# Hybrid decoder layer with a mixture of experts: expert rows written first as residual plus contribution, then added, through two row lists and three token buffers

## The chip, the cores and the metric

One core of one Trainium2 chip. The metric is the device time of one execution in microseconds (us), median of three runs. All arithmetic is float32. The engines are TensorE (PE in the profile, PEld its weight loads), VectorE (DVE), ScalarE (ACT), GpSimd (POOL) and SyncE (SP). Transfers are carried by the core's 16 DMA engines. SP issues the weight loads; POOL issues the indirect ones, whose row numbers lie in SBUF.

## What is computed

One layer on 512 tokens of width 1024: RMSNorm, one input projection whose columns feed a Mamba-2 head group and a forgetting-attention head group, an output projection, and a residual sum, called x2 here. Then the part that matters:

```python
g_star = jnp.argmax(grp_logits, axis=-1)               # one of 4 groups of 8 experts
top_val, top_idx = lax.top_k(sel, 2)                   # two experts of that group
w2 = jax.nn.softmax(top_val, axis=-1) * p_g
hid = silu(h @ w_gate[e]) * (h @ w_up[e])              # 1024 -> 256, for each chosen expert e
x = x2 + sum over the token's two experts of w2 * (hid @ w_down[e])
```

There are 32 experts with 3 MB of weights each. Every token has exactly two contributions, both from one group of eight experts.

## The kernel before, in words

**Up to the router.** x2 is made in blocks of 128 tokens (chunks). SP writes each chunk twice to DRAM: to `x2_dram`, from which rows are gathered, and to the output, to which contributions are added (lines 476 and 477). DVE routes the tokens (`route_group`, `route_first`, `route_second`, from line 1885): `i1` and `i2` are keys of a token's two experts (the larger key is the lower expert number), and `E12` is their one-hot form. Each expert has `CAP` = 64 slots. PE turns one-hot products into a token number for each slot (`slot_tokens`, line 1394) and DVE stores them as `slot_rows` (line 1965), with `NO_ROW`, out of bounds, where a slot is empty. PE then sums how many slots each expert holds (lines 1436 to 1438) and makes the gate weight and the norm scale of each slot (line 1445).

**The expert stage.** There are 16 pairs: pair p is expert p on partitions 0 to 63 and expert p + 16 on partitions 64 to 127. A pair's work is:

- `gather(p)` (POOL, line 682): 128 slot rows of 4 KB from `x2_dram` into one of two buffers of `xg`.
- `tokens_transpose(p)` (PE, line 1456), then `tokens_copy(p)` (ACT line 1017 and DVE line 1994) into `xgT`.
- `gate_up(p)` (PE, line 1483; lines 1472 for pairs 0 and 1): 32 matmuls. `gate(p)` (ACT, line 1024) and `gated(p)` (DVE, line 2001) make `hid`; `hid_transpose(p)` (PE, line 1492) and `hidT_store(p)` (DVE, line 2008) turn it.
- `down(p)` (PE, line 1507): 16 matmuls into PSUM banks 6 and 7.
- `rows_scale(p)`: ACT scales the front half of the result (line 1030) while DVE scales the back half (line 2014) into `yrow`.
- `scatter(p)` (POOL, line 698): adds the 128 rows to the output in DRAM. It waits until the scatter of pair p-1 has landed, since two pairs can hold the same token.

SP loads the weights: three buffers for gate and up (4 MB a pair, line 367), four for down (2 MB a pair, line 383). A load into a buffer waits for `gate_up` or `down` of the pair that used it last.

What sets the order is the program of each engine. PE's loop is written so (`AHEAD` is 12):

```python
for p in range(NPAIR):
    if p < AHEAD: gate_up(p + 1, p + 1)
    hid_transpose(p)
    if p < NPAIR - 2: tokens_transpose(p + 2, p % 2)
    down(p, p)
    if AHEAD <= p < NPAIR - 1: gate_up(p + 1, p + 1)
```

DVE does in a step `hidT_store(p)`, `gated(p+1)`, `tokens_copy(p+2)`, `rows_scale(p)`; from p = 12 `gated(p+1)` comes last. ACT does `gate(p+1)`, `tokens_copy(p+2)`, `rows_scale(p)`. POOL issues gathers 0 to 3, then in step p `gather(p+4)` and `scatter(p)`; `gather(p)` waits for `tokens_transpose(p-2)`, which frees its buffer. After the loop all engines read `most_i`, the fullest expert's count; more rounds of a slower loop would follow only if it were over 64.

Of the kernel before, what the change touches and what calls it, by code (L numbers as in the profile page):

```python
# [20 lines left out]
P = 128  # L21
# [24 lines left out]
NGU, NDN = 3, 4  # L46
# [36 lines left out]
def hybrid_layer(nc, x, norm_mix_w, w_in, conv_w, conv_b, dt_bias, a_log, d_skip, ssm_norm_w, q_norm_w, k_norm_w,  # L83
# [7 lines left out]
    with ExitStack() as ctx:  # L91
# [17 lines left out]
        def sem(name):  # L109
            if name not in sems:  # L110
# [7 lines left out]
                         [("dn1", [P, 2, 2, D], F32), ("gu1", [P, 2, 2, KC, DE], F32)]))  # L118
# [26 lines left out]
                         [("sg", [P, DE], F32), ("hid", [P, DE], F32), ("hidT", [P, 2, DE], F32), ("yrow", [P, 2, D], F32),  # L145
                          ("slot_rows", [P, NPAIR], I32), ("slot_scale", [P, 2, NPAIR], F32), ("slot", [P, 4, 4], I32)],
# [14 lines left out]
                         + [(n, [P, TC, H], F32) for n in ("ncum", "ecum", "dte", "etot")], [("turn", [P, NE], F32)]))  # L161
        sp, lf, cum, tot, ncum, ecum, dte, etot = (m[n] for n in ("sp", "lf", "cum", "tot", "ncum", "ecum", "dte", "etot"))
        turn = m["turn"]
# [22 lines left out]
        slot_rows, slot_scale = m["slot_rows"], m["slot_scale"]  # L186
        slot = m["slot"]
# [196 lines left out]

        def more_experts(eng, expert):
# [12 lines left out]
        def _(sp):  # L398
# [123 lines left out]
            for j in range(2):
                sp.wait_ge(sem(f"rows_out{j}"), 16 * (NPAIR // 2))
# [3 lines left out]
        def _(pool):  # L527
# [8 lines left out]
            def lows(first, end):  # L536
                for i in range(first, end):
                    if low_engine("w", i) == "pool":
# [5 lines left out]
                               pattern=[[-1, P]], channel_multiplier=1).then_inc(sem("const_ident"), 1)  # L544
            pool.memset(ones[:], 1.0).then_inc(sem("const_ones"), 1)
            lows(0, HL)

            pool.wait_ge(sem("const_ident"), 1)
            pool.wait_ge(sem("const_ones"), 1)

            pool.affine_select(out=tri[:], in_=ones[:], compare_op=ALU.is_ge, fill=0.0, base=0,
                               pattern=[[1, P]], channel_multiplier=-1).then_inc(sem("const_masks"), 1)

            pool.affine_select(out=stri[:], in_=ones[:], compare_op=ALU.is_gt, fill=0.0, base=0,
                               pattern=[[1, P]], channel_multiplier=-1).then_inc(sem("const_masks"), 1)
# [21 lines left out]
            last.then_inc(sem("const_masks"), 1)  # L577
# [64 lines left out]
            for n in range(N_SO, N_AO):  # L642
                for k in range(KC):
# [6 lines left out]
                    if n == N_AO - 1 and k == 0:  # L650
# [4 lines left out]
                               1.0 / P, None, ALU.mult).then_inc(sem("turn_set"), 1)  # L655
# [26 lines left out]
            def gather(p):  # L682

                j = p % 2
                if p >= 2:
                    pool.wait_ge(sem("xg_transposed"), p - 1)
                pool.indirect_dma_start(out=m["xg"][:, j, :], out_offset=None, in_=x2_dram[:, :],  # L687
                                        in_offset=bass.IndirectOffsetOnAxis(ap=slot_rows[:, p:p + 1], axis=0),
                                        bounds_check=T - 1, oob_is_err=False).then_inc(sem(f"xg_in{j}"), 16)
# [12 lines left out]
            def gather_more(p, r4, n, row):  # L702

                j, e = r4 % 2, p % NPAIR
                pool.wait_ge(sem("xg_transposed"), p - 1)
                pool.wait_ge(sem(f"rows_out{j}"), (p - j) * 8)
                pool.wait_ge(sem("y_scaled_act"), p - 1)
                pool.wait_ge(sem("y_scaled_dve"), p - 1)
# [12 lines left out]
            def scatter_more(p, r4, n):  # L721

                j = r4 % 2
                pool.wait_ge(sem(f"rows_out{1 - j}"), (p + j) * 8)
                pool.wait_ge(sem("y_scaled_act"), p + 1)
                pool.wait_ge(sem("y_scaled_dve"), p + 1)
# [10 lines left out]
            gather(3)  # L737
            for p in range(NPAIR):
                if p + 4 < NPAIR:
                    gather(p + 4)  # L740
                scatter(p)
            pool.wait_ge(sem("most_known"), 1)
            over_cap = pool.value_load(most_i[0:1, 0:1])
            with pool.If(over_cap > CAP):
# [7 lines left out]
                for j in range(2):  # L752
                    pool.wait_ge(sem(f"rows_out{j}"), 16 * (ROUNDS * NPAIR // 2))
# [3 lines left out]
        def _(act):  # L757
# [267 lines left out]

            def rows_scale(p, j, gates):
                act.wait_ge(sem("down_done"), p + 1)
                if not isinstance(p, int) or p >= 2:
                    act.wait_ge(sem(f"rows_out{j}"), (p - j) * 8)
                act.activation(m["yrow"][:, j, 0:BLK], ps[6][:], ACT.Copy, scale=gates).then_inc(sem("y_scaled_act"), 1)  # L1030
# [10 lines left out]
            for p in range(NPAIR):  # L1041
# [4 lines left out]
                rows_scale(p, p % 2, slot_scale[:, 0, p:p + 1])  # L1046
# [6 lines left out]
        def _(pe):  # L1053
            pe.wait_ge(sem("const_ident"), 1)
# [13 lines left out]
            def rstd_rows():  # L1068

                pe.wait_ge(sem("const_ones"), 1)  # L1070
# [78 lines left out]
            def small_cums():  # L1149
                pe.wait_ge(sem("logs_known"), 1)  # L1150
                pe.wait_ge(sem("const_masks"), 2)
                pe.wait_ge(sem("const_ones"), 1)
# [4 lines left out]
            def small_rows():  # L1157
                pe.wait_ge(sem("parts_known"), 1)
                pe.wait_ge(sem("const_masks"), 3)
# [215 lines left out]
            def ranks(c):  # L1375
# [4 lines left out]
                if c == 0:  # L1380
                    pe.wait_ge(sem("turn_set"), 1)
# [67 lines left out]
            def tokens_transpose(p, j):  # L1449
                pe.wait_ge(sem(f"xg_in{j}"), (p - j) * 8 + 16)  # L1450
# [3 lines left out]
                rows = m["xg"][:, j, :].rearrange("t (p k) -> t k p", k=KC)  # L1454
# [40 lines left out]
            def down(p, r4):  # L1495
# [3 lines left out]
                if not isinstance(p, int) or p >= 1:  # L1499
                    pe.wait_ge(sem("y_scaled_act"), p)  # L1500
                    pe.wait_ge(sem("y_scaled_dve"), p)
# [14 lines left out]

            tokens_transpose(0, 0)
            gate_up(0, 0)
            for p in range(NPAIR):
# [12 lines left out]
        def _(dve):  # L1532
# [432 lines left out]
            dve.tensor_scalar(slot_rows[:], ps[5][:, 0:NPAIR], float(NO_ROW), None, ALU.add).then_inc(sem("rows_known"), 1)  # L1965
            for k, at in ((0, i1), (1, i2)):
# [13 lines left out]
            dve.wait_ge(sem("slots_done"), 2)  # L1980
# [3 lines left out]
            dve.wait_ge(sem("ranks_done"), TC + 1)  # L1984
            dve.tensor_reduce(most[:], ps[6][:, 2 * NE:3 * NE], AX, ALU.max).then_inc(sem("dve_seq"), 1)
            dve.wait_ge(sem("dve_seq"), step())
            dve.tensor_copy(most_i[:], most[:]).then_inc(sem("most_known"), 1)
# [21 lines left out]

            def rows_scale(p, j, gates):  # L2010
                dve.wait_ge(sem("down_done"), p + 1)
                if not isinstance(p, int) or p >= 2:
                    dve.wait_ge(sem(f"rows_out{j}"), (p - j) * 8)
                dve.tensor_scalar(m["yrow"][:, j, BLK:], ps[7][:], gates, None, ALU.mult).then_inc(sem("y_scaled_dve"), 1)  # L2014
# [9 lines left out]
            gated(0, 0, slot_scale[:, 1, 0:1])  # L2024
            for p in range(NPAIR):
# [5 lines left out]
                rows_scale(p, p % 2, slot_scale[:, 0, p:p + 1])  # L2031
# [27 lines left out]
```

## Time and profile before

| what | value |
|---|---|
| time, median of 3 runs | 774.24 us (773.31 to 775.62) |
| the profiled execution: its own time | 774.24 us |
| its span, first to last instruction | 772.6 us |
| busy: PE, DVE, ACT, POOL | 709.6, 380.6, 279.3, 145.4 us |
| DMA bytes in the span | 150.31 MB |
| read from and written to HBM | 145.09 MB, 12.88 MB |
| expert stage, first gather issued | 519.5 us |
| last matmul of the last pair ends | 763.5 us |

Busy time is the sum over instructions of an engine; a busy PE is not PE at its peak, since matmuls overlap. PEclk is the share of its full clock that TensorE was granted. DMA share is the mean busy share of the 16 DMA engines. Times inside the trace count from the start of the span. In the list of instructions a bracket behind a row gives the engine's idle time before it and what ended it.

### The profile page before, as it was taken

Reading aid. Unit: us, or ns where it says so; the run is one execution under the profiler, and the core shown is the slowest. Engines: PE = TensorE matmul, PEld = TensorE weight load, DVE = VectorE, ACT = ScalarE, POOL = GpSimd, SP = SyncE. Lnnn points to the kernel's source line nnn. Section 1 sums busy time; section 2 is a strip of 40 time slices with the busy share of each in tenths; the row PEclk is TensorE's granted clock in tenths of the full one; section 3 lists DMA queues with packets and bytes.
Section 4 is the critical chain, followed back from the end, with each engine's and each line's share of the span. In section 5 each row is a group of like instructions: output and inputs, shape, how many; then the busy total and the mean of one; then the engine's idle time right before and its main releaser. Section 6 shows DMA issues by size and latency. Waiting matters only on the chain.

```text
span 772.6 us, 10496 instructions
## 1 busy us (share of the span) xinstructions
PE 709.6 (92%) x3892; PEld 476.4 (62%) x3892; DVE 380.6 (49%) x758; ACT 279.3 (36%) x648; POOL 145.4 (19%) x126
## 2 busy tenths in 40 slices
PE   6999999999999999999999999988999786868784
PEld 5867888788888888666566688876433232323221
DVE  6876777785868723766776553471212110111100
ACT  4934633544454445544554432221212110211100
POOL 3513331330301102000120032011122111111111
PEclk9999999999999999999999999977999898989988
DMA  8333212330303122500110059798999999999972
GB/s 279 84 110 109 92 36 93 108 95 14 108 3 109 53 88 78 212 8 1 52 59 2 1 197 419 316 375 316 407 402 404 393 407 416 404 413 408 387 281 42
DMA packets 44038, 150.31 MB, mean 195 GB/s; under 512 B 11557, under 2 KB 11649, under 8 KB 32209
## 3 DMA queue, kind: packets, MB, share of 16 engines
q1 hardware_dynamic: 38384, 134.61, 45.5%
q0 software_dynamic: 4720, 8.70, 4.6%
q10 hardware_dynamic: 880, 6.30, 2.0%
q8 instruction: 33, 0.54, 0.3%
q14 instruction: 21, 0.16, 0.1%
HBM read 145.09 MB, written 12.88 MB: 204 GB/s over the span
## 4 chain that ended last, share of the span: by engine, by line
PE 67%; SPq 15%; DVE 6%; DMA 6%; ACT 3%; issue 2%; POOL 0%; POOLq 0%; ACTq 0%; DVEq 0%
PE bank L1093 13%; PE bank L1095 12%; PE bank L1094 12%; SPq L367 10%; PE bank L1483 6%; SPq L383 4%; DMA s_gu<-in_w_expert_up_dram 4%; PE bank L1507 3%; PE bank L1330 3%; PE bank L1302 2%; PE bank L1316 2%; PE bank L1472 2%; DVE s_wl L261 2%; PE bank L1210 2%; PE bank L1306 1%
## 5 line engine op out<-in xcount | busy, mean ns | idle before, releaser
L1483 PE MATMUL bank<-s_gu,s_xgT 128*64 128x512 f32 x448 | 110.3, 649 | 29.7 <-DMA s_gu<-in_w_expert_up_dram 29.7
L261 DVE TENSOR_TENSOR s_wl<-s_raw,s_wh 128x512 fp32r<-128x512 f32 x84 | 88.5, 1092 | 25.9 <-ACT s_wh L772 25.6
L1483 PEld LDWEIGHTS bank<-s_gu,s_xgT 128*64 128x64 f32 x448 | 36.6, 149 | 102.2 <-issue 102.2
L772 ACT ACTIVATE s_wh<-s_raw 128x512 fp32r<-128x512 f32 x120 | 74.0, 630 | 41.6 <-PE bank L1095 18.4
L1093 PE MATMUL bank<-s_wh,s_hTh 128*128 128x512 f32 x192 | 78.7, 410 | 0.0
L261 POOL TENSOR_TENSOR s_wl<-s_raw,s_wh 128x512 fp32r<-128x512 f32 x36 | 53.5, 1498 | 131.7 <-ACT s_wh L772 131.1
L1095 PE MATMUL bank<-s_wh,s_hTl 128*128 128x512 f32 x192 | 75.0, 391 | 0.0
L1094 PE MATMUL bank<-s_wl,s_hTh 128*128 128x512 f32 x192 | 74.8, 390 | 0.0
L2008 DVE COPY s_hidT<-bank 128x256 f32<-128x256 f32 x16 | 6.8, 424 | 115.1 <-PE bank L1492 115.1
L1507 PE MATMUL bank<-s_dn,s_hidT 128*64 128x512 f32 x256 | 58.5, 598 | 1.0 <-DVE s_hidT L2008 1.0
L1024 ACT ACTIVATE s_sg<-bank,s_slot_scale 128x256 f32<-128x256 f32 x16 | 7.6, 473 | 138.0 <-PE bank L1483 129.1
L926 ACT ACTIVATE s_Pe<-bank,s_nmax 128x128 f32<-128x128 f32 (+3 forms) x64 | 33.6, 525 | 54.3 <-DVE s_nmax L1805 54.3
L698 POOL DMA_INDIRECT out_dram<-s_yrow,s_slot_rows x16 | 25.2, 1576 | 86.1 <-DVE s_yrow L2014 69.4
L1094 PEld LDWEIGHTS bank<-s_wl,s_hTh 128*128 128x128 f32 x192 | 36.1, 188 | 8.3 <-issue 1.4
L1093 PEld LDWEIGHTS bank<-s_wh,s_hTh 128*128 128x128 f32 x192 | 36.1, 188 | 8.2 <-issue 1.4
L1095 PEld LDWEIGHTS bank<-s_wh,s_hTl 128*128 128x128 f32 x192 | 36.0, 188 | 7.7
L687 POOL DMA_INDIRECT s_xg<-x_rows,s_slot_rows x16 | 16.6, 1037 | 122.5 <-PE bank L1456 119.0
L1093 PE MATMUL bank<-s_hTh,s_wh 128*128 128x512 f32 x96 | 38.4, 400 | 0.0
L1095 PE MATMUL bank<-s_hTh,s_wl 128*128 128x512 f32 x96 | 37.5, 391 | 0.0
L1094 PE MATMUL bank<-s_hTl,s_wh 128*128 128x512 f32 x96 | 37.4, 390 | 0.0
L1507 PEld LDWEIGHTS bank<-s_dn,s_hidT 128*64 128x64 f32 x256 | 17.0, 136 | 30.5 <-issue 27.4
L2014 DVE TENSOR_SCALAR s_yrow<-bank,s_slot_scale 128x512 f32<-128x512 f32 x16 | 12.0, 751 | 48.2 <-PE bank L1507 48.2
(280 smaller groups left out, 1338.4 us busy)
## 6 DMA issues: line engine op xcount, KB each, us to landing
s_dn<-in_w_expert_down_dram SPq DMA_DIRECT2D x30, 1024.0 KB, 23.8
s_gu<-in_w_expert_gate_dram SPq DMA_DIRECT2D x28, 1024.0 KB, 23.1
s_gu<-in_w_expert_up_dram SPq DMA_DIRECT2D x28, 1024.0 KB, 25.7
s_raw<-in_w_in_dram SPq DMA_DIRECT2D x88, 256.0 KB, 3.5
s_raw<-in_w_out_dram SPq DMA_DIRECT2D x32, 256.0 KB, 3.2
s_xin<-in_x_dram SPq DMA_DIRECT2D x4, 512.0 KB, 6.2
s_zs<-in_x_dram SPq DMA_DIRECT2D x1, 2048.0 KB, 10.4
s_gu<-in_w_expert_gate_dram ACTq DMA_DIRECT2D x2, 1024.0 KB, 11.1
```

The source lines that it names most:

```text
L261: eng.tensor_tensor(low, full, high.bitcast(F32), ALU.subtract).then_inc(sem(f"{what}_low_{low_engine(what, i)}"), 1)
L367: sp.dma_start(m[f"gu{b}"][:, half, which, :, :].rearrange("p k f -> p (k f)"), src).then_inc(sem(f"gu_in{b}"), 16)
L383: sp.dma_start(m[f"dn{b}"][:, half, :, :].rearrange("p k n -> p (k n)"), src).then_inc(sem(f"dn_in{b}"), 16)
L698: pool.indirect_dma_start(out=out[:, :], out_offset=bass.IndirectOffsetOnAxis(ap=slot_rows[:, p:p + 1], axis=0), in_=m["yrow"][:, j, :], i ...
L772: act.activation(wh[:, i % HL, :], raw[:, i % RAW, :], ACT.Copy).then_inc(sem("w_high"), 1)
L926: act.activation(Pe[:, v % 3, 0:n], ps[4 + v % 3][:, 0:n], ACT.Exp, bias=nmax[:, v:v + 1], accum_out=rsum[:, v:v + 1]).then_inc(sem("p_exp ...
L1093: pe.matmul(dst, ah, bh, start=start, stop=False)
L1094: pe.matmul(dst, ah, bl, start=False, stop=False)
L1095: return pe.matmul(dst, al, bh, start=False, stop=stop)
L1330: last = pe.matmul(ps[7][par * HD:(par + 1) * HD, qb * P:(qb + 1) * P], V[:, kb, h * HD:(h + 1) * HD], PT[:, par, kb * P:(kb + 1) * P], st ...
L1483: last = pe.matmul(ps[j][r, :].rearrange("p (w f) -> p w f", w=2), m["xgT"][:, j, k, r], gu[:, half, :, k, :], start=(k == 0), stop=(k == ...
L1507: last = pe.matmul(ps[6 + nb][r, :], m["hidT"][:, j, at:at + CAP], dn[:, half, q, nb * BLK:(nb + 1) * BLK], start=(q == 0), stop=(q == 1))
```

## The change

Instead of adding both contributions of a token to the output, the pair that holds a token's first contribution (the lower expert number) writes residual plus contribution plainly; the second contribution is added by a scatter as before.

- DVE marks which of a token's two experts is first (`is_first`, `E_first`); PE makes a second list of slot rows from it (16 matmuls of the kind of line 1399) where it counted slots before; the counting (`totals`) moves behind `gate_up(0)`.
- `rows_split` (DVE, after `gated(0)`) makes `first_rows`, `second_rows` and `holds_first`, a factor of 1 for the slots that hold a first contribution and 0 for the others.
- `keep_first(p)` (ACT) multiplies the gathered rows in place by `holds_first`. `rows_finish(p)` (DVE) then makes `yrow` = matmul result x gate + kept row, both halves one after the other. Pairs 7 and 15 hold no first contribution and keep `rows_scale`.
- `scatter(p)` issues a plain write by `first_rows` (14 pairs) and an adding one by `second_rows` (14 pairs; pairs 0 and 8 hold no second one).
- The gathered rows are needed until `rows_finish`, so there are three buffers, and `gather(p)` waits for the rows of pair p-3. POOL issues gathers 0 to 2, then `gather(p+3)` and `scatter(p)` in step p.

The core of the diff; the waits for constants merely share one semaphore, and the rare extra rounds get new counts:

```diff
             def gather(p):
-                j = p % 2
-                if p >= 2:
-                    pool.wait_ge(sem("xg_transposed"), p - 1)
-                pool.indirect_dma_start(out=m["xg"][:, j, :], out_offset=None, in_=x2_dram[:, :],
+                if p >= NXG:
+                    pool.wait_ge(sem("y_front"), p - NXG + 1)
+                    pool.wait_ge(sem("y_back"), p - NXG + 1)
+                pool.indirect_dma_start(out=token_rows(p), out_offset=None, in_=x2_dram[:, :],
...
             def scatter(p):
                 j = p % 2
                 if p:
-                    pool.wait_ge(sem(f"rows_out{1 - j}"), (p + j) * 8)
-                pool.wait_ge(sem("y_scaled_act"), p + 1)
-                pool.wait_ge(sem("y_scaled_dve"), p + 1)
-                pool.indirect_dma_start(out=out[:, :], out_offset=bass.IndirectOffsetOnAxis(ap=slot_rows[:, p:p + 1], axis=0),
-                                        in_=m["yrow"][:, j, :], in_offset=None, bounds_check=T - 1, oob_is_err=False,
-                                        compute_op=ALU.add).then_inc(sem(f"rows_out{j}"), 16)
+                    pool.wait_ge(sem(f"rows_out{1 - j}"), landed(p - 1))
+                pool.wait_ge(sem("y_front"), p + 1)
+                pool.wait_ge(sem("y_back"), p + 1)
+                if has_first(p):
+                    pool.indirect_dma_start(out=out[:, :], out_offset=bass.IndirectOffsetOnAxis(ap=first_rows[:, p:p + 1], axis=0),
+                                            in_=m["yrow"][:, j, :], in_offset=None, bounds_check=T - 1, oob_is_err=False)\
+                        .then_inc(sem(f"rows_out{j}"), 16)
+                if has_second(p):
+                    pool.indirect_dma_start(out=out[:, :], out_offset=bass.IndirectOffsetOnAxis(ap=second_rows[:, p:p + 1], axis=0),
+                                            in_=m["yrow"][:, j, :], in_offset=None, bounds_check=T - 1, oob_is_err=False,
+                                            compute_op=ALU.add).then_inc(sem(f"rows_out{j}"), 16)
...
             gather(2)
-            gather(3)
+            pool.wait_ge(sem("rows_known"), 3)
             for p in range(NPAIR):
-                if p + 4 < NPAIR:
-                    gather(p + 4)
+                if p + NXG < NPAIR:
+                    gather(p + NXG)
                 scatter(p)
...
+            def keep_first(p):
+                if p == 0:
+                    act.wait_ge(sem("rows_known"), 3)
+                act.wait_ge(sem("xg_transposed"), p + 1)
+                act.activation(token_rows(p), token_rows(p), ACT.Copy, scale=holds_first[:, p:p + 1]).then_inc(sem("first_kept"), 1)
...
-            pe.matmul(ps[6][:, 2 * NE:3 * NE], ones[:], turn[:], start=True, stop=False)
+            pe.wait_ge(sem("rows_known"), 2)
             for c in range(TC):
-                last = pe.matmul(ps[6][:, 2 * NE:3 * NE], ones[:], occ[:, c, :], start=False, stop=(c == TC - 1))
-            last.then_inc(sem("ranks_done"), 1)
+                for k in range(2):
+                    for half in range(2):
+                        last = pe.matmul(ps[7][half * CAP:(half + 1) * CAP, 0:NPAIR], pick_tok(c)[:, k, :],
+                                         E_first[:, k, c, half * NPAIR:(half + 1) * NPAIR], start=(c == 0 and k == 0), stop=(c == TC - 1 and k == 1))
+            last.then_inc(sem("slots_done"), 1)
...
             tokens_transpose(0, 0)
             gate_up(0, 0)
+            totals()
...
+            def rows_finish(p, j, gates):
+                dve.wait_ge(sem("down_done"), p + 1)
+                dve.wait_ge(sem("first_kept"), sum(has_first(q) for q in range(p + 1)))
+                if p >= 2:
+                    dve.wait_ge(sem(f"rows_out{j}"), landed_before(p, j))
+                for nb in range(2):
+                    cols = slice(nb * BLK, (nb + 1) * BLK)
+                    dve.scalar_tensor_tensor(out=m["yrow"][:, j, cols], in0=ps[6 + nb][:], scalar=gates, in1=token_rows(p)[:, cols],
+                                             op0=ALU.mult, op1=ALU.add).then_inc(sem("y_back" if nb else "y_front"), 1)
```

## Rows read from the trace of the kernel before

**Rows 1.** The page, part 2: the span in 40 slices of 19.3 us

```profile
PEclk9999999999999999999999999977999898989988
DMA  8333212330303122500110059798999999999972
```

**Rows 2.** Waits between 500 and 773 us: us in total, times, longest us

```profile
PE bank L1483 <- DMA s_gu<-in_w_expert_up_dram: 29.7, 7, 6.8
```

**Rows 3.** Chain that ended last: start us, us, what

```profile
583.43 6.89 PE bank L1483 x32
590.34 0.33 SPq L367
...
704.18 30.69 DMA s_gu<-in_w_expert_up_dram
735.00 10.07 PE bank L1483 x32
```

**Rows 4.** Instructions of PE in order of time: start us, us

```profile
547.92 7.04 PE L1483 MATMUL bank<-s_gu,s_xgT 128*64 128x512 f32 x32
...
555.23 1.06 PE L1456 MATMUL bank<-s_ident,s_xg 128*128 128x128 f32 x8
...
559.71 7.04 PE L1483 MATMUL bank<-s_gu,s_xgT 128*64 128x512 f32 x32
...
612.20 10.02 PE L1483 MATMUL bank<-s_gu,s_xgT 128*64 128x512 f32 x32 [5.21 <-DMA s_gu<-in_w_expert_up_dram]
...
629.36 7.09 PE L1483 MATMUL bank<-s_gu,s_xgT 128*64 128x512 f32 x32 [2.22 <-DMA s_gu<-in_w_expert_up_dram]
...
699.12 8.78 PE L1483 MATMUL bank<-s_gu,s_xgT 128*64 128x512 f32 x32 [2.52 <-DMA s_gu<-in_w_expert_up_dram]
...
717.57 7.04 PE L1483 MATMUL bank<-s_gu,s_xgT 128*64 128x512 f32 x32
...
726.04 1.06 PE L1456 MATMUL bank<-s_ident,s_xg 128*128 128x128 f32 x8
727.03 3.65 PE L1507 MATMUL bank<-s_dn,s_hidT 128*64 128x512 f32 x16
735.00 10.06 PE L1483 MATMUL bank<-s_gu,s_xgT 128*64 128x512 f32 x32 [4.32 <-DMA s_gu<-in_w_expert_up_dram]
...
750.65 7.04 PE L1483 MATMUL bank<-s_gu,s_xgT 128*64 128x512 f32 x32
```

**Rows 5.** The gathers, pairs 4 to 15 and pairs 0 and 1

```profile
L687 POOL DMA_INDIRECT s_xg<-x_rows,s_slot_rows x12: 988/1042/1047, 545.3 to 710.0; - x12
DMA to landing us min/median/max: 7.8/8.3/9.0
...
DMA to landing us min/median/max: 3.8/3.9/4.0
```

**Rows 6.** Instructions of DVE and POOL: start us, us

```profile
548.14 0.75 DVE L2014 TENSOR_SCALAR s_yrow<-bank,s_slot_scale 128x512 f32<-128x512 f32 x1 [2.90 <-PE bank L1507]
...
549.82 1.62 POOL L698 DMA_INDIRECT out_dram<-s_yrow,s_slot_rows x1 [3.55 <-DVE s_yrow L2014]
```

**Rows 7.** DVE line 1799, ACT line 1000: min/median/max ns, first and last start

```profile
L1799 DVE SCALAR_TENSOR_TENSOR s_zs<-bank,s_rs_a,s_zs x8: 737/751/751, 460.0 to 507.5; 128x512 f32<-128x512 f32 x8
...
L1000 ACT ACTIVATE s_wl<-s_zs x4: 1048/1058/1061, 482.0 to 509.5; 128x1024 fp32r<-128x1024 f32 x4
```

**Rows 8.** PE before the first pair: start us, us

```profile
517.62 0.61 PE L1399 MATMUL bank<-s_E,s_pick_tok 128*64 128x16 f32 x8 [0.34 <-DVE s_pick_tok L1925]
518.17 0.64 PE L1436 MATMUL bank<-s_turn,s_ones 128*128 128x32 f32 x2
518.62 1.89 PE L1438 MATMUL bank<-s_occ,s_ones 128*128 128x32 f32 x8
```

**Rows 9.** Stretches: us; PE, PEld, DVE, ACT, POOL busy; PEclk, DMA share, GB/s

```profile
596.00:600.00 4.00, 4.00 (x22) 1.34 (x20) 0.01 (x1) 0.00 (x0) 1.58 (x1) 1.00 1.03 422
600.00:604.00 4.00, 4.00 (x24) 1.98 (x22) 1.37 (x3) 1.02 (x4) 0.00 (x0) 1.00 1.02 357
...
748.00:752.00 4.00, 4.00 (x22) 1.35 (x20) 0.75 (x1) 0.69 (x1) 0.00 (x0) 1.00 0.27 113
```

More of the change, by code:

```diff
@@ L45 @@
 ROUNDS = T // CAP + 1
-NGU, NDN = 3, 4
+NGU, NDN, NXG = 3, 4, 3
 AHEAD = 12
@@ L383, in load_down, with token_rows, has_first, has_second @@
                 sp.dma_start(m[f"dn{b}"][:, half, :, :].rearrange("p k n -> p (k n)"), src).then_inc(sem(f"dn_in{b}"), 16)
+        def token_rows(p):
+            return m["xg"][:, p % NXG, :] if p % NXG < 2 else m["xg2"][:]
+        def has_first(p):
+            return p % NEG != NEG - 1
+        def has_second(p):
+            return p % NEG != 0
+        def landed(p):
+            return 16 * sum(has_first(q) + has_second(q) for q in range(p % 2, p + 1, 2))
+        def landed_before(p, j):
+            return landed(p - 2) if isinstance(p, int) else (p - j) * 8 + (landed(NPAIR - 1) - 8 * NPAIR)
         def more_experts(eng, expert):
@@ L576, in _ @@
                     pool.wait_ge(sem("pool_seq"), step())
-            last.then_inc(sem("const_masks"), 1)
+            last.then_inc(sem("consts"), 1)
             pool.iota(iota[:], [[1, CAP]], base=0, channel_multiplier=0, allow_small_or_imprecise_dtypes=True)\
@@ L705, in gather_more @@
                 pool.wait_ge(sem("xg_transposed"), p - 1)
[L706 to L708 removed]
+                pool.wait_ge(sem(f"rows_out{j}"), landed_before(p, j))
+                pool.wait_ge(sem("y_front"), p)
+                pool.wait_ge(sem("y_back"), p)
                 held(n)
@@ L1028, in rows_scale @@
                 if not isinstance(p, int) or p >= 2:
-                    act.wait_ge(sem(f"rows_out{j}"), (p - j) * 8)
-                act.activation(m["yrow"][:, j, 0:BLK], ps[6][:], ACT.Copy, scale=gates).then_inc(sem("y_scaled_act"), 1)
+                    act.wait_ge(sem(f"rows_out{j}"), landed_before(p, j))
+                act.activation(m["yrow"][:, j, 0:BLK], ps[6][:], ACT.Copy, scale=gates).then_inc(sem("y_front"), 1)
             def expert_more(p, r4):
@@ L1045, in _ @@
                     tokens_copy(p + 2, p % 2)
-                rows_scale(p, p % 2, slot_scale[:, 0, p:p + 1])
+                if has_first(p):
+                    keep_first(p)
+                else:
+                    rows_scale(p, p % 2, slot_scale[:, 0, p:p + 1])
                 if AHEAD <= p < NPAIR - 1:
@@ L1449, in tokens_transpose @@
             def tokens_transpose(p, j):
-                pe.wait_ge(sem(f"xg_in{j}"), (p - j) * 8 + 16)
+                if isinstance(p, int):
+                    pe.wait_ge(sem(f"xg_in{p % NXG}"), 16 * (p // NXG + 1))
+                    tokens = token_rows(p)
+                else:
+                    pe.wait_ge(sem(f"xg_in{j}"), (p - j) * 8 + (16 * len(range(j, NPAIR, NXG)) + 16 - 8 * NPAIR))
+                    tokens = m["xg"][:, j, :]
                 if not isinstance(p, int) or p >= 1:
@@ L1453, in tokens_transpose @@
                     pe.wait_ge(sem("xgT_dve"), p)
-                rows = m["xg"][:, j, :].rearrange("t (p k) -> t k p", k=KC)
+                rows = tokens.rearrange("t (p k) -> t k p", k=KC)
                 for k in range(KC):
@@ L1515, in expert_more, with totals @@
                 down(p, r4)
+            def totals():
+                pe.matmul(ps[6][:, 2 * NE:3 * NE], ones[:], turn[:], start=True, stop=False)
+                for c in range(TC):
+                    last = pe.matmul(ps[6][:, 2 * NE:3 * NE], ones[:], occ[:, c, :], start=False, stop=(c == TC - 1))
+                last.then_inc(sem("ranks_done"), 1)
             tokens_transpose(0, 0)
             gate_up(0, 0)
+            totals()
             for p in range(NPAIR):
@@ L1965, in _ @@
             dve.tensor_scalar(slot_rows[:], ps[5][:, 0:NPAIR], float(NO_ROW), None, ALU.add).then_inc(sem("rows_known"), 1)
+            dve.tensor_tensor(is_first[:, 0, :], i1, i2, ALU.is_gt).then_inc(sem("dve_seq"), 1)
+            dve.tensor_tensor(is_first[:, 1, :], i2, i1, ALU.is_gt).then_inc(sem("dve_seq"), 1)
+            step()
+            dve.wait_ge(sem("dve_seq"), step())
+            dve.tensor_tensor(E_first[:].rearrange("p k c e -> p (k c) e"), E12[:].rearrange("p k c e -> p (k c) e"),
+                              over(is_first[:].rearrange("p k c -> p (k c)"), P, 2 * TC, NE), ALU.mult).then_inc(sem("rows_known"), 1)
             for k, at in ((0, i1), (1, i2)):
@@ L1983, in _ @@
                 .then_inc(sem("payload_ready"), 1)
[L1984 to L1987, printed above, removed]
             dve.wait_ge(sem("scales_in_slots"), 1)
@@ L2008, in hidT_store, with rows_split, most_slots @@
                 dve.tensor_copy(m["hidT"][:, j, :], ps[4][:, 0:DE]).then_inc(sem("hidT_stored"), 1)
+            def rows_split():
+                dve.tensor_scalar(first_rows[:], ps[7][:, 0:NPAIR], float(NO_ROW), None, ALU.add).then_inc(sem("dve_seq"), 1)
+                dve.tensor_scalar(holds_first[:], ps[7][:, 0:NPAIR], 0.0, None, ALU.is_lt).then_inc(sem("dve_seq"), 1)
+                dve.tensor_scalar(first_away[:], ps[7][:, 0:NPAIR], 0.0, float(NO_ROW), ALU.is_lt, ALU.mult).then_inc(sem("dve_seq"), 1)
+                step()
+                step()
+                dve.wait_ge(sem("dve_seq"), step())
+                dve.scalar_tensor_tensor(out=second_rows[:], in0=ps[5][:, 0:NPAIR], scalar=float(NO_ROW), in1=first_away[:],
+                                         op0=ALU.add, op1=ALU.add).then_inc(sem("rows_known"), 1)
+            def most_slots():
+                dve.wait_ge(sem("ranks_done"), TC + 1)
+                dve.tensor_reduce(most[:], ps[6][:, 2 * NE:3 * NE], AX, ALU.max).then_inc(sem("dve_seq"), 1)
+                dve.wait_ge(sem("dve_seq"), step())
+                dve.tensor_copy(most_i[:], most[:]).then_inc(sem("most_known"), 1)
+            def rows_finish(p, j, gates):
[7 more added lines that the diff above has]
+                                             op0=ALU.mult, op1=ALU.add).then_inc(sem("y_back" if nb else "y_front"), 1)
             def rows_scale(p, j, gates):
@@ L2024, in _ @@
             gated(0, 0, slot_scale[:, 1, 0:1])
+            rows_split()
+            most_slots()
             for p in range(NPAIR):
@@ L2030, in _ @@
                     tokens_copy(p + 2, p % 2)
-                rows_scale(p, p % 2, slot_scale[:, 0, p:p + 1])
+                if has_first(p):
+                    rows_finish(p, p % 2, slot_scale[:, 0, p:p + 1])
+                else:
+                    rows_scale(p, p % 2, slot_scale[:, 0, p:p + 1])
                 if AHEAD <= p < NPAIR - 1:
```

61 lines of the change are left out of this document (31 added, 30 removed).

## The prediction, made before the changed kernel ran

> **What bounds the kernel now.** The page's slices come first. Slices 29 to 38 of 40 (541 to 734 us) all stand at 9 tenths or more of DMA share, so the expert stage is a stream of weights [rows 1]. The waits say the same from PE's side: PE waits 29.7 us for gate and up weights, in 7 waits [rows 2]. The chain that ended last says where it turns: up to 583 to 590 us it runs through PE's matmuls, then through SP's queue, which can't issue faster than the DMA engines drain, until the weights of pair 14 land at 735.0; from there the tail is PE's again [rows 3]. The order of PE's instructions gives two paces. While weights lie ready, a pair takes 559.71 - 547.92 = 11.8 us. Later `gate_up` starts when its weights land, (735.00 - 612.20)/7 = 17.5 us a pair [rows 4]. So between 612 and 735 PE has 5.7 us of slack in each pair, and only DMA time counts. The gathers sit in neither path: POOL issues each one step before PE wants it, and it takes 8.3 us to land [rows 5].
>
> Span 772.6 us, its own time 774.24, which is also the median: I add 1.6 us to a span.
>
> **The change part by part.**
>
> *Less DMA work.* A scatter that adds must read its destination. POOL's 1.58 us between 596 and 600 us is a scatter being issued; in the next 4 us the stream carried 357 GB/s instead of 422 [rows 9]: 65 GB/s x 4 us = 0.26 MB, which is 64 rows of 4 KB, a pair's mean (1024 contributions over 16 pairs). The 512 first contributions lose that reading: 2.1 MB at 0.42 MB/us = 5.0 us of DMA time, nearly all of it before pair 14's weights. Bounds: 0, if a plain write takes as long, and 5.0. The 12 more scatters carry mostly empty slots; their price isn't shown apart, and the dip is used up by the real rows, so I take 0. At most each costs another such dip, 0.26/0.42 = 0.6 us, 7 us in all. All this counts only while DMA sets the pace.
>
> *Before the first pair.* PE's ten counting matmul records (0.64 + 1.89 us) give way to 32 of the kind that took 0.61 us for 8, so 2.4 us, about the same; they return behind `gate_up(0)`, at twice the clock in about 1.1 us (they took 2.3 from the first's start to the last's end) [rows 8]. Small DVE instructions come ahead of the gate weights; the bound covers them. The first gathers are issued as before, and PE's transposes wait for them. I take +1.1 us on PE: `gate_up(2)` starts at 549.0, not 547.92. Bounds 0 and 2.5. Gather 2 is issued earlier and needed later, 0.
>
> *ACT.* `keep_first` is 128x1024, by the row of that size 1.06 us [rows 7], behind `tokens_copy` while PE does `down`, 3.65 us. It ends first; 0. If that cover went, it would add up to 1.06 us a pair, and more would wait for it, as follows.
>
> *POOL.* A step now issues a gather (1.04 us) and up to two scatters (1.6 us each) [rows 5, 6]: 4.2 us out of 15 or more, and `scatter(p)` waits for the landing of p-1, issued a whole step earlier. 0, unless the second scatter lands so late that the next gather queues behind it (below).
>
> *The new wait, which decides.* Now `gather(p+2)` waits until the rows of p-1 are made. Behind it stand, in this order, `tokens_transpose(p+2)`, `down(p)`, the rows of p, and the next gather: a loop, once round per pair. It was open before, since the gather waited for a transpose two pairs back. Its price, from one `gate_up` start (that is when `down` of the pair before is through) to the next:
>
> 1. `down` to DVE's start: 548.14 - 547.92 = 0.2 us [rows 4, 6].
> 2. Rows on DVE alone, both halves: 2 x 0.75 = 1.5 us [rows 7]. Before, ACT did one half beside it.
> 3. DVE's end to POOL's indirect DMA: 549.82 - 548.89 = 0.9 us [rows 6].
> 4. The gather, 8.3 us in a full DMA stream; bounds 3.8 (empty engines) and 9.0 [rows 5]. The stream stays full, so 8.3.
> 5. Transpose and `down`: 559.71 - 555.23 = 4.5 us [rows 4].
>
> Sum 15.4, and some 0.1 of semaphores: 15.5 us a pair instead of 11.8. `gate_up` and the `hid` transpose cover 555.23 - 547.92 = 7.3 us of the first four; PE then stands still for 3.7 us in every pair.
>
> *What the stall does to TensorE's clock.* Idle times of 2.52 and 4.32 us ahead of `gate_up` were followed by one of 8.78 and 10.06 us, against 7.04 at full clock, 2.4 GHz; after 2.22 us there was no loss (7.09) [rows 4]. 3.7 us lies between those that lost 1.7 and 3.0 us to the half clock. Here the transpose and `down` run straight behind the stall, in the loop. I take 1.7 us in three pairs of four, 1.3 us a pair, since short stalls don't always lower the clock. Bounds 0 and 3.0. The loop: 15.5 + 1.3 = 16.8 us.
>
> The Trainium skill, "TensorE: Matmul & The Clock Gate" (HAM oscillation — how this bites in real kernels), has a rule against this change: a loop in which PE waits for a DMA in each trip starts each trip throttled. The rows above agree for single waits; none shows a wait in every trip.
>
> **The sum.** `gate_up` starts behind `down(0)` at 549.0; twelve loops later, with pair 7's half beside ACT (-0.75), `gate_up(13)` starts at 549.0 + 12 x 16.8 - 0.75 = 749.9, against 717.57 before. The slower loop is just under the DMA pace, so the load order keeps running; SP's buffer waits come later, yet its queue had some 20 us of backlog (30.69 us from issue to landing in rows 3). The stream ends about 748 as before [rows 9], or 5 us earlier, and the last gather meets idle engines (3.8 us): PE's own path is longer, 726.04 - 717.57 = 8.5 us to the transpose and 4.6 us to the end of `down(13)`, 763.0 [rows 4]. From `gate_up(14)` to `gate_up(15)` it was 15.65 us with a slow one of 10.06; at full clock 12.6, so 775.6. Behind that start lay 772.6 - 750.65 = 21.95 us: span 797.5, time 799.1 us. The 5 us of DMA time saved are lost to the wait.
>
> **Rivals.**
>
> *A. The loop without a clock loss.* 15.5 us: `gate_up(13)` at 734.3; the last gather is still in the full stream, `down(13)` ends at 749.9; + 12.6 + 21.95 = 784.4, time 786. For: one idle of 2.22 us cost nothing. Against: 2.52 did.
>
> *B. The loop hides, and the change gains.* This is the other side. It needs the loop at 14.6 us or less, which is where the end comes out even: (772.6 - 21.95 - 12.6 + 0.75 - 549.0)/13; so a gather of 7.4 us without clock loss. Below that PE meets the weights in time, and DMA sets the end: 774.2 - 5.0 = 769.2. For: gathers in idle engines took 3.9, and half of the adding falls away. Against: not one of twelve in the stream took less than 7.8, with scatters far from them too.
> The Trainium skill, "DMA: Bandwidth & Descriptors" (Anatomy of one DMA — SWDGE (gpsimd) path), puts a DMA at about 2 us and its bytes over 436 GB/s, 2.6 us for a gather; by that this rival would be the result. The measured 8.3 decides against it.
>
> *C. The gather queues behind the two scatters,* or the clock is lost in full (3.0 us): 18.5 us a loop gives 549.0 + 222 - 0.75 + 13.1 + 12.6 + 21.95 = 817.9, time 819.5. Against: past 17.5 us a pair the weight stream gets gaps, and a gather in a gap is faster; so it is held near 812.
>
> *D. Plain writes save nothing* (the change doesn't do what it says). That alters only B, to 774.
>
> **Numbers.** Forecast 0.60, A 0.22, C 0.05; B 0.08; something between B and A that comes out even 0.05. Range: from 781 (A with 0.4 us less per loop) to 812 (C). A measurement of this kernel can tell 0.3%, 2.3 us. Slower 0.87, same 0.05, faster 0.08.
>
> **What would show it.** Right: gathers preceded by a wait for DVE's line of `rows_finish`, PE's transposes waiting 3 to 4 us for the gather in nearly every pair from pair 3 on, a PEclk below full in most stretches after 550, the weights of pair 14 landing well before PE asks, HBM reads down by 2.1 MB. PE's wait for weights, 29.7 us, would be all but gone. Wrong: `gate_up` still preceded by weight waits near 612 and 735, or gathers landing in under 7.4 us. If the gathers wait but the clock stays full, it is A; if the transposes wait over 5 us, C.

## The result: 802.5 us, 3.6% slower, and the profile after

| | before | after |
|---|---|---|
| time, median of 4 runs each | 774.93 us | 802.53 us (800.90 to 803.23) |
| ratio to before, 95% interval | | 1.0357 (1.0335 to 1.038) |
| the profiled execution: its own time, span | 774.24, 772.6 us | 800.9, 799.3 us |

The forecast was 799.1 us in a range of 781 to 812. One of the six runs of the kernel of experiment 1, below, took 1777 us, for a reason that no trace shows; its ratio leaves that run out. The page of the changed kernel, its head, the rows of slices and the HBM counts:

```profile
span 799.3 us, 10607 instructions
...
PEclk9999999999999999899999999969988999898798
DMA  8333321230311331400200199879999999999412
...
HBM read 145.09 MB, written 19.17 MB: 206 GB/s over the span
```

The DMA row is full to slice 37 (740 us) and then falls to 4, 1 and 2: the weights are in before 750 us, and the kernel runs 50 us longer. Before, the stream ended at about 748 us [rows 9], 24 us ahead of the end. Two rows of the list of waits between 500 and 800 us (us in total, times, longest):

```profile
POOL s_xg L706 <- DVE s_yrow L2087: 169.4, 12, 29.2
...
PE bank L1497 <- DMA s_xg<-x_rows,s_slot_rows: 43.9, 12, 10.0
```

The wait for weights, 29.7 us before [rows 2], is no longer in the list. In its place PE's transposes wait for the gather, twelve times, and the gather waits for the rows that DVE finishes. Two trips round that loop, in the chain that ended last (start us, us, what):

```profile
604.55 0.75 DVE s_yrow L2087
605.42 0.53 issue
606.16 8.37 DMA s_xg<-x_rows,s_slot_rows
614.57 1.20 PE bank L1497 x8
615.77 5.22 PE bank L1548 x16
621.05 0.63 issue
621.68 0.75 DVE s_yrow L2087
623.28 7.80 DMA s_xg<-x_rows,s_slot_rows
```

Rows finished, POOL's reaction, gather, transposes, `down`, and again. `down` took 5.22 us there; in full clock it takes 3.65 [rows 4]. The same in the order of PE's instructions (start us, us; idle time before and its end in brackets), which answers to [rows 4]:

```profile
553.12 7.04 PE L1524 MATMUL bank<-s_gu,s_xgT 128*64 128x512 f32 x32
560.09 0.51 PE L1533 MATMUL bank<-s_ident,s_hid 128*128 128x128 f32 x2
564.40 1.97 PE L1497 MATMUL bank<-s_ident,s_xg 128*128 128x128 f32 x8 [3.80 <-DMA s_xg<-x_rows,s_slot_rows]
566.30 4.37 PE L1548 MATMUL bank<-s_dn,s_hidT 128*64 128x512 f32 x16
570.50 7.03 PE L1524 MATMUL bank<-s_gu,s_xgT 128*64 128x512 f32 x32
...
647.83 1.16 PE L1497 MATMUL bank<-s_ident,s_xg 128*128 128x128 f32 x8 [2.96 <-DMA s_xg<-x_rows,s_slot_rows]
648.91 3.65 PE L1548 MATMUL bank<-s_dn,s_hidT 128*64 128x512 f32 x16
652.40 7.04 PE L1524 MATMUL bank<-s_gu,s_xgT 128*64 128x512 f32 x32
...
744.86 1.97 PE L1497 MATMUL bank<-s_ident,s_xg 128*128 128x128 f32 x8 [9.99 <-DMA s_xg<-x_rows,s_slot_rows]
746.76 4.58 PE L1548 MATMUL bank<-s_dn,s_hidT 128*64 128x512 f32 x16
751.18 7.03 PE L1524 MATMUL bank<-s_gu,s_xgT 128*64 128x512 f32 x32
...
764.13 7.04 PE L1524 MATMUL bank<-s_gu,s_xgT 128*64 128x512 f32 x32
...
776.76 7.04 PE L1524 MATMUL bank<-s_gu,s_xgT 128*64 128x512 f32 x32
```

From `gate_up(2)` to `gate_up(13)` there are twelve trips. They took (751.18 - 553.12)/12 = 16.5 us each, and (717.57 - 547.92)/12 = 14.1 us before, a mean of PE's own pace on a stock of loaded weights and of the weights' pace after it. That is where the time went: 5.2 us by the start of `gate_up(2)`, 28.4 us in the twelve trips, and 6.9 us given back behind `gate_up(13)`, since the weights that PE had to wait for in the end before are now long there (48.1 us to the end instead of 55.0). Together 26.7 us, the difference of the spans.

POOL in one step (start us, us; idle before):

```profile
606.16 1.05 POOL L706 DMA_INDIRECT s_xg<-x_rows,s_slot_rows  x1 [12.12 <-DVE s_yrow L2087]
607.52 1.01 POOL L718 DMA_INDIRECT out_dram<-s_yrow,s_first_rows  x1 [0.31 <-issue]
608.84 1.59 POOL L722 DMA_INDIRECT out_dram<-s_yrow,s_second_rows  x1 [0.30 <-issue]
```

The line of the gathers, pairs 3 to 14, which answers to [rows 5]:

```profile
DMA to landing us min/median/max: 7.6/7.9/8.1
```

The two scatters, of which one is new, take POOL 2.6 us of a step in which it then idles for 12. They stand behind the gather, and no gather took longer for them.

### The profile page after: what moved, and what is told of

Its sections match the earlier page's. It is cut to its first block, busy times and chain, and to the rows that moved or that the text cites. A ratio compares the mean times of both kernels' runs of the same rounds, so it can differ in the third digit from the quotient of the medians.

```text
span 799.3 us, 10607 instructions
## 1 busy us (share of the span) xinstructions
PE 719.0 (90%) x3924; PEld 479.2 (60%) x3924; DVE 390.8 (49%) x779; ACT 284.4 (36%) x648; POOL 156.9 (20%) x138
## 3 DMA queue, kind: packets, MB, share of 16 engines
HBM read 145.09 MB, written 19.17 MB: 206 GB/s over the span
## 4 chain that ended last, share of the span: by engine, by line
PE 71%; DMA 14%; DVE 8%; issue 3%; ACT 3%; POOL 0%; SPq 0%; POOLq 0%; ACTq 0%; DVEq 0%
PE bank L1126 13%; DMA s_xg<-x_rows,s_slot_rows 12%; PE bank L1128 12%; PE bank L1127 12%; PE bank L1548 9%; PE bank L1497 3%; PE bank L1363 3%; PE bank L1524 3%; PE bank L1335 2%; PE bank L1513 2%; PE bank L1349 2%; DVE s_wl L263 2%; PE bank L1243 2%; PE bank L1339 1%; DMA s_raw<-in_w_in_dram 1%
## 5 line engine op out<-in xcount | busy, mean ns | idle before, releaser
L1524 PE MATMUL bank<-s_gu,s_xgT 128*64 128x512 f32 x448 | 98.5, 592 | 0.0
L796 ACT ACTIVATE s_wh<-s_raw 128x512 fp32r<-128x512 f32 x120 | 74.0, 630 | 43.5 <-DMA s_raw<-in_w_in_dram 19.3
L1548 PE MATMUL bank<-s_dn,s_hidT 128*64 128x512 f32 x256 | 71.3, 708 | 1.0 <-DVE s_hidT L2059 1.0
L1524 PEld LDWEIGHTS bank<-s_gu,s_xgT 128*64 128x64 f32 x448 | 31.9, 137 | 64.3 <-issue 64.3
L1497 PE MATMUL bank<-s_ident,s_xg 128*128 128x128 f32 x128 | 22.8, 333 | 43.9 <-DMA s_xg<-x_rows,s_slot_rows 43.9
L1497 PEld LDWEIGHTS bank<-s_ident,s_xg 128*128 128x128 f32 x128 | 18.6, 202 | 46.7 <-DMA s_xg<-x_rows,s_slot_rows 46.1
L1041 ACT ACTIVATE s_xgT<-bank,s_wpk 128x128 f32<-128x128 f32 x64 | 18.3, 368 | 79.0 <-PE bank L1497 79.0
L2087 DVE SCALAR_TENSOR_TENSOR s_yrow<-bank,s_slot_scale,s_xg 128x512 f32<-128x512 f32 x28 | 19.7, 746 | 53.3 <-PE bank L1548 53.3
L1548 PEld LDWEIGHTS bank<-s_dn,s_hidT 128*64 128x64 f32 x256 | 20.0, 163 | 41.4 <-issue 39.0
L2045 DVE TENSOR_TENSOR s_xgT<-bank,s_wpk 128x512 f32<-128x512 f32 x16 | 11.1, 692 | 59.9 <-PE bank L1497 59.9
```

The source lines that it names most:

```text
L796: act.activation(wh[:, i % HL, :], raw[:, i % RAW, :], ACT.Copy).then_inc(sem("w_high"), 1)
L1041: last = act.activation(m["xgT"][:, j, k, :], ps[2][:, k * P:(k + 1) * P], ACT.Copy, scale=wpk[:, k:k + 1])
L1497: last = pe.transpose(ps[2 + k // 4][:, (k % 4) * P:(k % 4 + 1) * P], rows[:, k, :], ident[:])
L1524: last = pe.matmul(ps[j][r, :].rearrange("p (w f) -> p w f", w=2), m["xgT"][:, j, k, r], gu[:, half, :, k, :], start=(k == 0), stop=(k == ...
L1548: last = pe.matmul(ps[6 + nb][r, :], m["hidT"][:, j, at:at + CAP], dn[:, half, q, nb * BLK:(nb + 1) * BLK], start=(q == 0), stop=(q == 1))
L2087: dve.scalar_tensor_tensor(out=m["yrow"][:, j, cols], in0=ps[6 + nb][:], scalar=gates, in1=token_rows(p)[:, cols], op0=ALU.mult, op1=ALU.a ...
```

## The experiments

Each is compared with the kernel before, run on the same chip, which took 774.57 us beside experiments 1 to 4 and 774.33 beside 5 to 7. The changed kernel was not run beside them: what is compared with its 802.53 us, or with times of the other group, goes across separate measurements.

**1. The gather waits only for the kept rows.** ACT writes the kept rows into `yrow`, DVE adds into it in place, and the gather's buffer is free as soon as that copy is made.

```diff
 def gather(p):
-    pool.wait_ge(sem("y_front"), p - NXG + 1)
-    pool.wait_ge(sem("y_back"), p - NXG + 1)
+    pool.wait_ge(sem("xg_transposed"), p - NXG + 1)
+    pool.wait_ge(sem("first_kept"), sum(has_first(q) for q in range(p - NXG + 1)))
...
 def keep_first(p):
-    act.activation(token_rows(p), token_rows(p), ACT.Copy, scale=holds_first[:, p:p + 1])
+    if p >= 2:
+        act.wait_ge(sem(f"rows_out{p % 2}"), landed_before(p, p % 2))
+    act.activation(m["yrow"][:, p % 2, :], token_rows(p), ACT.Copy, scale=holds_first[:, p:p + 1])
...
 def rows_finish(p, j, gates):
-    dve.scalar_tensor_tensor(..., in1=token_rows(p)[:, cols], ...)
+    dve.scalar_tensor_tensor(..., in1=m["yrow"][:, j, cols], ...)
```

> The changed kernel, but ACT writes the kept rows into yrow and the gather waits only for that, not for the finished rows. Theory (the wait of the gather for the finished rows closes a loop that sets the pace): the loop is open again, the weights set the pace, and the 5.0 us of DMA time saved show: 770 us (768 to 773). Rival 1 (more scatters, the rows on DVE alone, or the added work before the first pair set the time): stays near 800. Rival 2 (the loop is open, but plain writes save nothing): 775.

Measured 771.82 us, ratio 0.9966 (0.9953 to 0.9979); once more, beside experiments 5 to 7:

> The version whose gather waits only for the kept rows, unchanged, once more beside the others of this call, as the measure for the one with earlier kept rows: 771.8 us as before (770.5 to 773).

771.14 us, ratio 0.9953 (0.9936 to 0.997). All the lists, scatters, kept rows and DVE's double work are in this kernel, and it is 31 us faster than the changed one. So none of them costs this by itself; what made the loss is the place of the wait, which put them into the loop. Its PE waits for weights again (from the order of PE's instructions, first profile):

```profile
643.34 9.52 PE L1526 MATMUL bank<-s_gu,s_xgT 128*64 128x512 f32 x32 [4.75 <-DMA s_gu<-in_w_expert_up_dram]
...
713.01 1.97 PE L1499 MATMUL bank<-s_ident,s_xg 128*128 128x128 f32 x8 [7.52 <-DMA s_xg<-x_rows,s_slot_rows]
714.91 4.44 PE L1550 MATMUL bank<-s_dn,s_hidT 128*64 128x512 f32 x16
719.19 7.03 PE L1526 MATMUL bank<-s_gu,s_xgT 128*64 128x512 f32 x32
```

One long wait for a gather is left, that of pair 14.

**2. The late gather alone, in the kernel before.** Two buffers suffice for it.

```diff
 def gather(p):
     if p >= 2:
         pool.wait_ge(sem("xg_transposed"), p - 1)
+    if p >= 3:
+        pool.wait_ge(sem("y_scaled_act"), p - 2)
+        pool.wait_ge(sem("y_scaled_dve"), p - 2)
...
 gather(2)
-gather(3)
 for p in range(NPAIR):
-    if p + 4 < NPAIR:
-        gather(p + 4)
+    if p + 3 < NPAIR:
+        gather(p + 3)
```

> The kernel before with one part of the change alone: the gather of pair p also waits for the scaled rows of pair p-3 (POOL issues gather p+3 and scatter p in step p); no lists, no kept rows, no plain writes. Theory: the loop is the whole loss; it is 0.7 us shorter than in the changed kernel since ACT and DVE share the rows: 0.2+0.75+0.9+8.0+0.1+4.5 and 1.4 of clock = 15.9 us a pair, gate_up(13) at 547.9+12x15.9=738.7, and 788 us in all (783 to 793). Rival (the loss lies in the added scatters and DVE work): 775.

Measured 787.66 us, ratio 1.0165 (1.0135 to 1.0196). With nothing else of the change, the wait costs 13 us. Its trips, from the order of PE's instructions:

```profile
549.16 7.04 PE L1485 MATMUL bank<-s_gu,s_xgT 128*64 128x512 f32 x32
...
737.54 7.03 PE L1485 MATMUL bank<-s_gu,s_xgT 128*64 128x512 f32 x32
```

188.4/12 = 15.7 us, against 16.5 in the changed kernel. Of the 0.8 us between them, DVE's second half of the rows is 0.66 (1.41 against 0.75) and the clock 0.34: it cost some 1.7 us in seven of the twelve trips here and in ten there. The gathers of the loop, 8.1 us here and 7.9 there (medians), take 0.2 off. Between the two profiles, 788.0 and 799.3 us long, the twelve trips are 9.7 us; `gate_up(2)` begins 4.0 us later in the changed kernel (553.12 against 549.16), of which 2.4 stand ahead of the first transposes already (526.64 against 524.24), and its tail is 2.3 us shorter. The medians, 787.66 and 802.53, lie further apart, by 14.9 us; the four runs here spread over 6 us.

**3. Filler for PE while it waits.** Matmuls of constants into an unused bank.

```diff
 hid_transpose(p)
+if 1 <= p <= 12:
+    if p == 1:
+        pe.wait_ge(sem("rows_known"), 3)
+    for _ in range(40 if p == 12 else 12):
+        pe.matmul(ps[5][:, 0:P], ones[:], ident[:], start=True, stop=True)
 if p < NPAIR - 2:
     tokens_transpose(p + 2, p % 2)
 down(p, p)
```

> The changed kernel with 12 idle matmuls (40 in step 12) ahead of the transposes of pairs 3 to 14, some 2.6 us of work (9 in step 12) where PE would stand still for the gather. Theory (each stall costs 1.7 us of half clock in the loop): transposes and down take 4.5 us instead of 6.2 in ten of twelve loops, so 12 x 1.45 = 17 us less: 785 us (781 to 790). Rival (the clock's loss falls in cover of the gather and costs nothing): 802 us, or more if the filler itself comes into the path.

Measured 788.76 us, ratio 1.0183 (1.0168 to 1.0198): 13.8 us less, by adding work. First the changed kernel, then the one with filler, in the same stretch (us; busy of PE, PEld, DVE, ACT, POOL; PEclk, DMA share, GB/s):

```profile
560.00:720.00 160.00, 129.66 (x564) 49.02 (x564) 28.51 (x49) 26.18 (x60) 30.70 (x26) 0.91 1.02 410
```

```profile
560.00:720.00 160.00, 152.11 (x851) 75.79 (x849) 29.20 (x50) 28.37 (x65) 33.98 (x28) 1.00 1.02 414
```

The granted clock is 1.00 instead of 0.91, and the order of PE's instructions shows `down` back at its length:

```profile
550.58 7.04 PE L1524 MATMUL bank<-s_gu,s_xgT 128*64 128x512 f32 x32
...
577.31 1.16 PE L1497 MATMUL bank<-s_ident,s_xg 128*128 128x128 f32 x8 [1.39 <-DMA s_xg<-x_rows,s_slot_rows]
578.40 3.65 PE L1548 MATMUL bank<-s_dn,s_hidT 128*64 128x512 f32 x16
...
735.49 7.04 PE L1524 MATMUL bank<-s_gu,s_xgT 128*64 128x512 f32 x32
```

A trip takes 184.9/12 = 15.4 us, 1.1 less. Transposes and `down` take 4.57 us in all twelve trips, against a mean of 5.96: the clock gave 1.4 us, nearly the 1.45 expected. Some came back elsewhere, since the gathers took 8.4 us here (median) and not 7.9.

**4. Plain writes turned into adds, in the kernel with the early gather.**

```diff
 in_=m["yrow"][:, j, :], in_offset=None, bounds_check=T - 1, oob_is_err=False,
+compute_op=ALU.add,
```

> As the first kernel of this call, but the scatter of first contributions adds too instead of writing plainly, so its sums hold the residual twice. Theory (the reading of the destination is real DMA time and shows once the weights set the pace): 5 us over the first kernel, about 775 us. Rival (plain writes and adds cost the stream the same): no difference.

Measured 778.40 us, ratio 1.0047 (1.0031 to 1.0063): 6.6 us over its twin. The two intervals are 0.5% to 1.1% apart, 4 to 8.5 us, so the forecast 5.0 is inside. The stream itself, first with plain writes, then with adds only:

```profile
560.00:720.00 160.00, 133.92 (x618) 51.96 (x615) 31.53 (x54) 28.37 (x65) 38.68 (x32) 0.94 1.02 414
```

```profile
560.00:720.00 160.00, 131.93 (x610) 51.32 (x608) 31.74 (x55) 28.84 (x66) 42.23 (x31) 0.94 1.02 404
```

414 against 404 GB/s at the same full share: 2.5% of a stream of some 200 us, 5 us.

The same run shows what the rest of the change costs once the loop is open. This kernel adds as many rows as the kernel before and takes 3.8 us more (778.40 against 774.57). Some 2.5 of them are likely the last gather's wait (experiment 7). What the 12 more scatters cost is not shown apart: in the window above the kernel before has 406 GB/s against 404 here, which over 200 us is 1 us. So the change as meant saves 5 to 6.6 us, and experiment 1 keeps 2.8 of them.

**5. The same edit in the changed kernel.**

> The changed kernel with its first contributions added instead of written plainly (its sums hold the residual twice); the lists, waits and buffers stay. Theory (the loop of gather, transposes, down and rows sets the pace, so the DMA time saved by plain writes is hidden): 802 to 804 us, like the changed kernel. Rival (the saved DMA time is in the changed kernel's 802.5 us too): 808 us, 6 more, as the version with the early gather showed.

Measured 801.27 us, ratio 1.0341 (1.032 to 1.0363), against 1.0357 (1.0335 to 1.038) with plain writes: no difference; the intervals allow for 4.6 us less and 2.2 us more, and not for 6 more. What is worth 6 us once the weights set the pace is worth nothing inside the loop.

**6. The scatters first, then the gather.**

```diff
 for p in range(NPAIR):
+    scatter(p)
     if p + NXG < NPAIR:
         gather(p + NXG)
-    scatter(p)
```

> The changed kernel with POOL's two lines of a step exchanged: scatter p, then gather p+3. The gather is issued 3.2 us later (1.0 + 1.6 and two gaps of 0.3). Theory (it lies in the loop, once per pair): 11 x 3.2 = 35 us more if the gather takes as long; past 17.5 us a pair the weight stream gets gaps and gathers land faster, so 830 us (822 to 840). Rival (the wait is mostly hidden): under 810 us.

Measured 830.73 us, ratio 1.074 (1.0696 to 1.0784), 28 us more for one exchange of two lines on an engine that is busy a fifth of the time. POOL's step, and the gathers' time to land over all pairs:

```profile
608.30 1.02 POOL L718 DMA_INDIRECT out_dram<-s_yrow,s_first_rows  x1 [15.68 <-DVE s_yrow L2087]
609.63 1.59 POOL L722 DMA_INDIRECT out_dram<-s_yrow,s_second_rows  x1 [0.30 <-issue]
611.52 1.05 POOL L706 DMA_INDIRECT s_xg<-x_rows,s_slot_rows  x1 [0.30 <-issue]
```

```profile
DMA to landing us min/median/max: 3.5/6.3/10.8
```

The gather is issued 3.2 us later. From pair 3 on gathers took 4.0 to 10.8 us to land, 6.7 in the median: the fast ones are as expected once the weight stream has gaps (5.8 us for the one issued at 632.15, with a DMA share of 0.89), the slow ones were not expected (10.8 us for the one issued at 649.93, in a full stream). A trip took 19.0 us ((777.05 - 549.03)/12, the starts of `gate_up(2)` and `gate_up(13)`), 2.5 more than in the changed kernel.

**7. The kept rows of pairs 11 and 12 one step earlier.** The kernel of experiment 1, aimed at its last long wait.

```diff
+if p + 1 in (11, 12):
+    if p + 1 == 11:
+        keep_first(10)
+    keep_first(p + 1)
+elif p in (11, 12):
+    pass
-if has_first(p):
+elif has_first(p):
     keep_first(p)
```

> The version whose gather waits only for the kept rows, with the kept rows of pairs 11 and 12 made one step earlier. In its profile PE stood 7.5 us for the gather of pair 14, in the step that has no gate_up ahead of the transposes, and from there PE's own work set the end. Theory (that stall is what is left of the loss): the transposes of pair 14 wait under 1 us, gate_up(14) meets its weights near 729, 3 us less: 769 us. Rival (the weights land no earlier than PE comes anyway): no difference from 771.8.

Measured 768.64 us, ratio 0.9929 (0.991 to 0.9948), 2.5 us under its twin, measured beside it; the two intervals overlap slightly, so the sign is likely and not certain. The reason was only half right. POOL, then PE:

```profile
698.01 1.59 POOL L722 DMA_INDIRECT out_dram<-s_yrow,s_second_rows  x1 [0.30 <-issue]
699.91 1.05 POOL L706 DMA_INDIRECT s_xg<-x_rows,s_slot_rows  x1 [0.30 <-issue]
```

```profile
712.08 1.93 PE L1505 MATMUL bank<-s_ident,s_xg 128*128 128x128 f32 x8 [4.21 <-DMA s_xg<-x_rows,s_slot_rows]
...
747.98 3.65 PE L1532 MATMUL bank<-s_gu,s_xgT 128*64 128x512 f32 x16 [0.53 <-DMA s_gu<-in_w_expert_up_dram]
```

The transposes of pair 14 still wait 4.2 us, not under 1. Their gather is issued 4.6 us earlier than in experiment 1's first profile (699.91 against 704.55), but right behind the two scatters of pair 10, and takes 12.1 us to land and not 8.4. That it hardly matters is in the last row: the second half of `gate_up(15)` waits for its weights, so this kernel ends with the stream. It is the fastest of all, 6 us under the kernel before.

## Why the prediction was right, step by step

**The wait that decides** was the right one. Experiment 2 has it alone (+13 us), experiment 1 has all but it (-3 us), and experiment 6 makes its loop longer (+28 us). Rival B, the loop hidden, fell: the loop took 16.5 us where it needed 14.6. It nearly came true in experiment 1, once the loop was open: 771.82 and 771.14 us, against its 769.2.

**The terms of the loop**, forecast and measured: rows on DVE 1.5 and 1.41 us; DVE's end to POOL 0.9 and, from 605.30 to 606.16, 0.86; the gather 8.3 and 7.9; transposes and `down` at full clock 4.5 and, where the clock held, 4.57; the clock's loss 1.3 and 1.4. For the last: ten of twelve trips took 6.1 to 6.3 us from the transposes' start to the next `gate_up` (or `hid` transpose), two took 4.57 and 4.58. So the loss was 1.7 us each time it came, as forecast, and it came in ten of twelve trips and not in nine. Rival A, no loss, fell with that, and experiment 3 shows the loss to be in the path. The sum was 16.8 and came out at 16.5.

**The stall** was forecast as 3.7 us. Eleven of the twelve were 2.5 to 3.8 (the twelfth, 10 us, is the step with no `gate_up` ahead of its transposes): the gather was shorter by 0.4 and the rows by 0.1. Even 2.54 us of standing still was followed by a slow `down` of 5.35 us, while the two trips without loss had stood still for 2.96 and 2.90: these rows give no length that decides.

**Rival C**, the gather behind the scatters or the whole 3.0 us of clock, fell: the gather goes first in POOL's step, and the loss was 1.7 us a time. But its cap, the 812 us of the range, was not sound. It rested on faster gathers in the gaps of the stream; experiment 6, which does put the gather behind the scatters, had 19.0 us a trip and 830.73 us.

**The start** was forecast at 549.0 us and lay at 553.12. 3.3 us of this is not the added work: the first transposes began at 526.64 instead of 523.30 us, and 3.2 of that stood already at PE's last `slot_tokens` (520.82 and 517.62), ahead of it. Over the profiles of this study that point lies between 522.0 and 526.6 us, with and without the change (the twin of experiment 1: 524.6; its first profile: 522.0). The rest is mine: from there to `gate_up(2)` it took 26.5 us and not 24.6, so the added work before the loop cost 1.9 us and not 1.1. That lies within the bounds of 0 and 2.5.

**The tail**: `gate_up(13)` to `gate_up(14)` 13.1 and 12.95 us, to `gate_up(15)` 12.6 and 12.63, to the end 21.95 and 22.5. PE did not wait for the last gather: it was issued at 753.67, when the stream had ended.

**The saved DMA time** was right in size and in being hidden: 5.0 us forecast, 5 in the stream's rates and 6.6 us in the times (experiment 4), nothing in the changed kernel (experiment 5). Rival D fell. The 12 more scatters were taken at 0; by the rates beside experiment 4 they cost some 1 us of the stream, within the bound of 7.

**Wrong** was one of the signs: I expected the page's count of HBM reads to fall by 2.1 MB. It stayed at 145.09 MB. See below.

The errors in the sum, +4.1 us at the start, -2.8 in the twelve trips, -0.15 and +0.6 in the tail, partly cancel; that the span came out only 1.8 us off owes something to this, and so to luck, since most of the +4.1 is where this one profile's first part ended. The median is 3.4 us off.

## What to carry to other kernels

When a buffer must live longer, look at what its release now waits for, and whether that closes a ring: here one more use of the gathered rows put a gather, PE and DVE into one loop, and the third buffer didn't open it. Add up the ring once, compare it with the pace of whatever bounds the stage, and count the clock that the new stalls cost. Copying the data away early, on an engine with time to spare, opened the ring; it took the place of a scaling of the same size.

## What the runs showed of the hardware

The page's count of HBM writes follows the shape of the transfers, not the rows that move. From before to after, written bytes rose from 12.88 to 19.17 MB, which is 12 scatters x 128 rows x 4 KB = 6.29 MB, though no more rows are written. The read count stayed at 145.09 MB in all kernels, whether they add or write plainly, so it holds nothing of the reading that an add does. The stream's rate told the truth instead: 414 against 404 GB/s.

Issuing a plain indirect scatter costs POOL 1.0 us, an adding one 1.6 us.

In a full weight stream a gather took 7.6 to 9.0 us to land in the two kernels compared, against 3.8 to 4.0 with idle DMA engines. Issued 0.3 us behind two scatters, it took 12.0 to 12.2 us, three times out of three in experiment 7. An early place in POOL's program is worth little if scatters stand just ahead of it.

Useless matmuls made a kernel 13.8 us faster, since PE's stalls of 2.5 to 3.8 us, once in 16.5 us, drew the granted clock down nearly every time. The Trainium skill, "TensorE: Matmul & The Clock Gate" (HAM oscillation — how this bites in real kernels), describes a loop in which every trip starts throttled after its wait for a DMA. The trace agrees in part: ten of twelve trips lost clock, but only three began at half the clock (transposes of 1.97 us). In four of the ten the transposes still ran at full clock, 1.16 us, and the loss came in `down`: behind the stall that ended at 597.43 the granted clock was 1.00 to 598.5 and 0.50 from there to 601.
